# Samples' products with C in four bursts, and half of the state updates behind the next group's first block

## The reference

```python
cum = jnp.cumsum(dt * A, axis=1)
y = jnp.einsum('btsgh,bsghp->btghp', w, x)
y = y + jnp.einsum('btgn,bghpn->btghp', cm, h) * jnp.exp(cum)[..., None]
tail = jnp.exp(cum[:, -1:] - cum) * dt
h_new = jnp.exp(cum[:, -1])[..., None, None] * h + jnp.einsum('bsgh,bsgn,bsghp->bghpn', tail, bm, x)
```

## Time and profile before

| | before |
|---|---|
| median of 3 runs | 1644.11 us (1643.53 to 1644.78) |
| profiled execution | 1640.79 us, span 1639.1 us, clock 0.926 |
| PE busy | 1396.7 us (85%) |
| DVE busy | 1198.9 us (73%) |
| ACT busy | 810.0 us (49%) |
| POOL busy | 214.6 us (13%) |
| block products, line 794 | 3840 records, 293.1 + 280.1 + 279.6 us |

### The profile page before, as it was taken

One profiled execution on the slowest core, in us unless ns is written; L12 is line 12 of the kernel. 1 busy time (PEld: TensorE's weight loads), 2 busy tenths in 40 slices (PEclk: granted clock), 3 DMA queues, 4 the chain that ended last, 5 costly groups with the idle time before them and its releaser, 6 DMA issues. The chain is left out here.

```text
span 1639.1 us, 26283 instructions
## 1 busy us (share of the span) xinstructions
PE 1396.7 (85%) x8709; PEld 1238.2 (76%) x8709; DVE 1198.9 (73%) x1710; ACT 810.0 (49%) x1420; POOL 214.6 (13%) x342
## 2 busy tenths in 40 slices
PE   3899989899998999989893899997349999999980
PEld 2898988888888798888882799985247777777760
DVE  4248787988878888787986454542639999999974
ACT  3136353554635436352541332322038989898961
POOL 0003011030211203012030000000220111111112
PEclk9999998999989899998995999998669999999995
DMA  5033441615325153351632825311269999999936
GB/s 146 19 110 81 117 127 53 186 56 144 98 86 151 52 156 86 103 139 53 171 84 78 272 70 172 113 52 36 91 253 369 366 359 363 356 369 358 364 140 231
DMA packets 191359, 271.53 MB, mean 166 GB/s; under 512 B 15884, under 2 KB 154358, under 8 KB 174886
## 3 DMA queue, kind: packets, MB, share of 16 engines
q1 hardware_dynamic: 178350, 245.62, 45.3%
q0 software_dynamic: 9968, 18.25, 3.1%
q10 hardware_dynamic: 2992, 7.03, 1.2%
HBM read 237.95 MB, written 50.26 MB: 176 GB/s over the span
## 5 line engine op out<-in xcount | busy, mean ns | idle before, releaser
L794 PE MATMUL pu<-xh,wh 128*128 128x304 f32 (+1 forms) x1280 | 293.1, 312 | 31.7 <-DVE wl L236 29.2
L794 PE MATMUL pu<-xl,wh 128*128 128x304 f32 (+1 forms) x1280 | 280.1, 302 | 0.0
L794 PE MATMUL pu<-xh,wl 128*128 128x304 f32 (+1 forms) x1280 | 279.6, 301 | 0.0
L794 PEld LDWEIGHTS pu<-xh,wh 128*128 128x128 f32 x1280 | 208.6, 200 | 47.3 <-DVE wl L236 36.2
L794 PEld LDWEIGHTS pu<-xl,wh 128*128 128x128 f32 x1280 | 208.7, 199 | 0.0
L794 PEld LDWEIGHTS pu<-xh,wl 128*128 128x128 f32 x1280 | 207.0, 199 | 0.0
L914 DVE SCALAR_TENSOR_TENSOR cacc<-a_p,gc,cacc 128x528 f32<-128x528 f32 x232 | 188.9, 814 | 5.8
L2086 DVE TENSOR_TENSOR W13l<-W,W13h 128x1024 fp32r<-128x1024 f32 x160 | 185.0, 1218 | 5.1 <-ACT W13h L2034 5.1
L496 ACT ACTIVATE wh<-ring 128x1024 fp32r<-128x1024 f32 x80 | 84.4, 1056 | 201.9 <-PE pu L794 201.9
L2034 ACT ACTIVATE W13h<-W 128x1024 fp32r<-128x1024 f32 x160 | 156.3, 1063 | 4.8 <-DMA W<-in_exp_w 4.8
L1993 PE MATMUL eh<-W13h,xch 128*128 128x512 f32 x320 | 130.5, 408 | 19.3 <-DVE xcl L2086 14.9
(11 more groups left out here) (397 smaller groups left out, 2694.2 us busy)
## 6 DMA issues: line engine op xcount, KB each, us to landing
W<-in_exp_w SPq DMA_DIRECT2D x120, 1024.0 KB, 7.7
ring<-in_w_in SPq DMA_DIRECT2D x80, 512.0 KB, 4.0
stage<-decay_rows SPq DMA_DIRECT2D x8, 1120.0 KB, 6.8
x<-in_state_ssm SPq DMA_DIRECT2D x16, 512.0 KB, 6.3
out_new_ssm_sample<-x SPq DMA_DIRECT2D x16, 512.0 KB, 5.3
wraw<-in_ssm_out_w SPq DMA_DIRECT2D x8, 1024.0 KB, 8.0
Ed<-decay_rows SPq DMA_DIRECT2D x32, 140.0 KB, 7.2
gates<-gbuf ACTq DMA_DIRECT2D x16, 280.0 KB, 2.1
```

The source lines that it names most:

```text
L794: last = pe.matmul(u_cols(r, a, b), w[:, k % RING, j, :], x[:, j, a:b], start=(j == 0 and n == 0), stop=(j == KD - 1 and n == 2))
```

## The change

1. The 16 products of the samples' states with C leave `stage2(5)`. A new `samples(r)` makes them in four bursts of four, each waiting for its own quarter of `h0T` alone; between bursts stands one of the 8 steps of block 9. The last burst tells VectorE. `block` gets bounds in steps instead of halves.
2. `states_added` for quarters 2 and 3 moves from the end of a group into `closing`, behind the next group's block 0. VectorE's updates of these quarters move behind its split of block 2's weights.
3. In the last group VectorE makes the samples' convolution and two taps before the first updates, with `cv` as room, and five more taps before `scaled`.

```diff
             def closing(g):
 
+                for r in (2, 3):
+                    states_added(g, r)
                 pe.wait_ge(s_y, 6 * g + 6 + 1)
...
-                    if ci == 0:
-                        pe.wait_ge(s_h0tev, 4 * g + 4)
-                        for i in range(2):
-                            for b in range(NSAMP):
-                                last = pe.matmul(pC[:, P * i + TSAMP * b:P * i + TSAMP * b + TSAMP],
-                                                 h0T[:, i, b, :], cv[:, 3, TSAMP * b:TSAMP * b + TSAMP],
-                                                 start=True, stop=True)
...
+                def samples(r):
+
+                    i, q = r // 2, r % 2
+                    pe.wait_ge(s_h0tev, 4 * g + r + 1)
+                    if r == 0:
+                        pe.wait_ge(s_y, 6 * g + 6)
+                    for b in range(4 * q, 4 * q + 4):
+                        c = P * i + TSAMP * b
+                        last = pe.matmul(pC[:, c:c + TSAMP], h0T[:, i, b, :], cv[:, 3, TSAMP * b:TSAMP * b + TSAMP],
+                                         start=True, stop=True)
+                    if r == 3:
+                        last.then_inc(s_pe2, 1)
...
-                block(9, (0,))
+                block(9, 0, 2)
                 states_turned(2)
+                block(9, 2, 4)
                 states_turned(3)
+                samples(0)
+                block(9, 4, 5)
+                samples(1)
+                block(9, 5, 6)
                 stage2(5)
-                block(9, (1,))
-                for r in range(4):
-                    states_added(r)
+                samples(2)
+                block(9, 6, 7)
+                samples(3)
+                block(9, 7)
+                for r in (0, 1):
+                    states_added(g, r)
...
                 split(g, 2)
+                if not is_first:
+                    states_new(g - 1, (2, 3))
...
-                for r in range(4):
-                    dve.wait_ge(s_hs, 4 * g + r + 2)
-                    dve.wait_ge(s_h0t, 4 * g + 4)
-                    for b in range(4):
-                        bb, i = 4 * (r % 2) + b, r // 2
-                        last = stt(h0[:, i, bb, :], h0[:, i, bb, :],
-                                   Ed[:, i, TSAMP * bb + TSAMP - 1:TSAMP * bb + TSAMP],
-                                   turn[r % 2][:, P * b:P * b + P])
-                    last.then_inc(s_hnew, 1)
+                if is_last:
+                    conf_samples(g, cv[:, :, :].rearrange("p q t -> p (q t)"))
+                    conf_taps(g, range(CK - TRAIL, CK - TRAIL + 2))
+                states_new(g, (0, 1))
...
             group(G - 1, is_last=True)
+            states_new(G - 1, (2, 3))
+            conf_taps(G - 1, range(CK - TRAIL + 2, CK - TRAIL + 7))
             scaled(G - 1)
-            conf_samples(G - 1)
-            conf_taps(G - 1, range(CK - TRAIL, CK))
+            conf_taps(G - 1, range(CK - TRAIL + 7, CK))
```

More of the change, by code:

```diff
@@ L756, in _, with states_added @@
             pe.wait_ge(s_dect, 4)
+            def states_added(g, r):
+                pe.wait_ge(s_Bblk, g + 1)
+                if r < 2:
+                    pe.wait_ge(s_h0tev, 4 * g + r + 3)
+                else:
+                    pe.wait_ge(s_hnew, 4 * g + r)
+                i, q = r // 2, r % 2
+                pe.matmul(turn[r % 2][:, :], xtl[0:SAMP, 1, 2 * i:2 * i + 2, :],
+                          Bblk[:, 4 * q:4 * q + 4, :], start=True, stop=True).then_inc(s_hs, 1)
             def closing(g):
+                for r in (2, 3):
+                    states_added(g, r)
                 pe.wait_ge(s_y, 6 * g + 6 + 1)
@@ L782, in free, with block @@
                     pe.wait_ge(s_ufree, U0 + max(r, 1))
-                def block(k, halves=(0, 1)):
+                def block(k, first=0, end=KD):
                     r = U_OF[k]
[L787 to L797, removed]
+                    if first == 0:
+                        free(r)
+                        low_done(pe, g, k)
+                    for j in range(first, end):
+                        for n, (w, x) in enumerate(((wh, xh), (wh, xl), (wl, xh))):
+                            for a, b in ((0, USPLIT), (USPLIT, T)):
+                                last = pe.matmul(u_cols(r, a, b), w[:, k % RING, j, :], x[:, j, a:b],
+                                                 start=(j == 0 and n == 0), stop=(j == KD - 1 and n == 2))
+                    if end == KD:
+                        last.then_inc(s_u, 1)
                 def stage1(j):
@@ L875, in group @@
                     block(k)
[L877 removed]
+                block(6, 0, 4)
                 stage1(0)
                 stage1(1)
[L880 removed]
+                block(6, 4)
                 stage2(0)
                 stage1(2)
[L883 removed]
+                block(7, 0, 4)
                 stage2(1)
                 stage1(3)
[L886 removed]
+                block(7, 4)
                 stage2(2)
                 stage1(4)
[L889 removed]
+                block(8, 0, 4)
                 stage2(3)
@@ L1016, in conf_taps, with states_new, conf_samples @@
                             k.link(ins)
-            def conf_samples(g):
-                    dve.wait_ge(s_yn, 2 * g + 2 + 1)
+            def states_new(g, rs):
+                for r in rs:
+                    dve.wait_ge(s_hs, 4 * g + r + 2)
+                    dve.wait_ge(s_h0t, 4 * g + 4)
+                    for b in range(4):
+                        bb, i = 4 * (r % 2) + b, r // 2
+                        last = stt(h0[:, i, bb, :], h0[:, i, bb, :],
+                                   Ed[:, i, TSAMP * bb + TSAMP - 1:TSAMP * bb + TSAMP],
+                                   turn[r % 2][:, P * b:P * b + P])
+                    last.then_inc(s_hnew, 1)
+            def conf_samples(g, room=None):
+                    if room is None:
+                        dve.wait_ge(s_yn, 2 * g + 2 + 1)
+                        room = ybuf[:, :, :].rearrange("p i t -> p (i t)")
                     n = CK - 1 + TSAMP
```

20 lines of the change are left out of this document (6 added, 14 removed).

## The result

| | predicted | measured |
|---|---|---|
| median | 1648.8 us (1635 to 1660) | 1661.59 us (1661.12 to 1662.49, 4 runs) |
| against before on the same chip (1643.82 us) | +4.7 us | +17.8 us, ratio 1.011 [1.0092, 1.0127] |
| profiled execution | 1645.5 us | 1661.39 us, span 1659.7 us, clock 0.906 (before 0.926) |

The changed kernel is slower, as forecast, but by nearly four times as much (1.1%), and 1.6 us beyond the range. The waits of TensorE in the groups' body come first, by instruction and what ended them: us in total, times, longest.

What follows compares the result with a forecast made beforehand. The hand-over between groups was taken to set the period: seven stretches at 31.3 us instead of 29.6 add 11.9, the last group's end saves 7.2, so +4.7: 1645.5 us profiled, median 3.3 above, 1648.8 us (1635 to 1660).

Steps and rivals of the forecast that it cites:

- What bounds the kernel: Hand-over between groups, from block 9's start to the next block 1: seven stretches of 29.6 us, 207.19 in all.
- The bursts: Samples' products with C between pieces of block 9: 0.91 us each, the 0.39 us wait gone, no clock fall.
- S: Moment when the last burst of samples' products ends, forecast 10.5 us after block 9's start.
- The wait of block 0: TensorE waits before the next group's block 0 for ScalarE to take the last gate: 2.4 us, new.
- The wait of the sums: TensorE waits before its two sums for VectorE's moved updates, behind block 0: 1.9 us more.
- The end: VectorE's work alone after the last group's last burst: 27.4 us, net 7.2 us less.
- The clock: Falls at the two new waits cost 2.9 us a stretch, making it 31.3 us, 1.7 more than before.
- Together 2.9: Clock price per stretch in us: 1.9 in block 0 every group, plus 1.0 for the second wait's fall half the time.
- a wait of 2.5 us alone was enough: Before the change, one TensorE wait of 2.5 us for weights was read as enough to bring the clock down.
- Rival C: Clock falls inside the bursts as well: price 4.9 us, 33.3 a stretch, +18.7, 1662.8 us; chance 0.12.
- Rival A: Clock holds through bursts, mostly falling inside waits: price 0.9 us a stretch, -9.3, 1634.8 us; chance 0.28.
- Rival B: Costs and gains cancel: clock price 2.2 us a stretch, no net change, 1644 us; chance 0.20.

Runs made afterwards that it cites:

- f3: In effect the changed kernel run again, as the intended fill ahead of the sums stands nowhere in the trace: 1660.14 us, ratio 1.0101 to before.
- f2: Changed kernel with 18 unread products of 256 columns (2.42 us) filling the wait ahead of block 0: 1647.09 us, ratio 1.0025 to before.
- g1: Changed kernel with 13 unread products of 256 columns (1.80 us) filling the wait ahead of the sums: 1653.37 us, ratio 1.0058 to before.
- f1: In effect f2 again, a second fill missing from the trace: 1645.66 us, one slow run at 1725.39 left out, ratio 1.0021 to before.
- g2: Changed kernel with unread products filling both waits, ahead of block 0 and ahead of the sums: 1656.68 us, ratio 1.0057 to before.
- e7: Changed kernel with VectorE's moved updates set ahead of its split of block 2: 1640.64 us, ratio 0.9974 to before.
- e2: Kernel before with part 2 alone, plus part 1's separate waits for each quarter ahead of the 16 products: 1644.03 us, ratio 0.9998.
- e1: Changed kernel without part 2, all state products and updates back at the group's end: 1629.96 us, ratio 0.9911; repeated 1628.12 us, 0.9901.
- e4: Changed kernel with block 0 of a next group waiting for its own bank alone: 1643.3 us, ratio 0.9989 to before.
- e6: e4 with state products 2 and 3 behind block 0's second and fourth eighth, all updates at the group's end: 1643.99 us, ratio 1.0003.
- e5: Changed kernel with the edits of both e4 and e7: 1626.87 us, ratio 0.988 to before; repeated 1633.48 us, 0.9933.
- part 3 alone: Kernel before with only VectorE's new order in the last group: 1635.54 us, ratio 0.9949 to before.

## Why the prediction was right in direction and wrong in size

**What bounds the kernel: right.** The hand-over between groups sets the period. Its seven stretches grew by 22.6 us (229.75 against 207.19), most of the 25.7 that the seven groups lost. The middle of a group kept its waits (29.3 us in 14, for 29.2), but not its clock; see below.

**The bursts: right.** No idle time ahead of them, full clock between them, S at 10.56 us for 10.5.

**The wait of block 0: right.** 2.38 for 2.4 us, released by ScalarE's gate, in six of seven; in the first stretch 0.26 was left, as the clock fell ahead of it and the state products took its time. **The wait of the sums: right.** 1.77 for 1.9. VectorE's split ended later (1.23 us from 387.65 on), the updates behind it.

**The end: right.** 27.3 us for 27.4. The last group's block 9 starts 24.5 us later than before (849.15 to 873.63) and the last tap ends 17.3 later (894.22 to 911.51), so the end gave back 7.2 us, the number forecast.

**The clock: this step failed.** The term "Together 2.9" had three faults of size.

| | forecast | in the stretch of the rows above |
|---|---|---|
| fall at the first wait, paid in block 0 | 1.9 us | 8.96 - 6.28 = 2.7 us |
| fall at the second wait, paid in the sums | "half the time the same price, 1.0" | 3.50 - 1.68 = 1.8 us, every time |
| low clock in block 1, behind the stretch | nothing | about 1.1 us, every time (69.5 for 68.4) |

So 4.5 us stands in the stretch where 2.9 was set: 28.3 + 4.5 = 32.8 us, as measured. Behind it another 1.1, which the sum could not see, as the stretch was cut at block 1's start. (The 2.4 us of 394.50:396.90 at half the clock do half their work, so 1.2 us is the upper bound of that share.) Part of this was made up: before, three of the seven pieces behind a stretch lost 1.5 us to the fall behind a wait for weights, and none does now, so these pieces grew by 3.1 us together, not by 7.7.

The whole account, in the two profiled executions: the stretches are 10.7 us longer than forecast (22.6 for 11.9), the pieces behind them 3.1, group 0 comes to its block 9 1.2 us earlier (157.30 for 158.50), and the end is as forecast. That is 12.6 us too little at the last tap, and the forecast of the median was 12.8 too low. The profiled execution came out 15.9 above its forecast; 3.3 us of that lie behind the last tap, where the change touches nothing, and the traced execution of before was itself 3.0 us under its median.

That the clock falls in the second wait was the least certain link, and I priced it by a mean over happening and not happening. It happened seven times of seven, and in the repeat (f3) again. What speaks for the waits as its cause is that filling them, at the same length, took the fall at that place away, in seven of seven stretches of f2 and g1 (six in f1). What speaks against a simple rule is that the fall then came elsewhere, in g1 and g2 as a longer low stretch from the bursts on, and that in the changed kernel itself, and in four groups of e7, the first fall stood ahead of the wait. The prediction's reading that a wait of 2.5 us alone was enough took one place: of the 14 waits for weights seven are of 2.5 us, and in the profiled executions three of these seven have a fall behind them before the change, none after it, and all seven in e2. The step also took "no fall" for the bursts and the work right behind them: that held in six of seven stretches here, and in two of seven of e1.

**Rival C** had the time right (1662.8) and the mechanism wrong: its fall inside the bursts isn't there, they run at 1.00. **Rival A** had the clock hold; it fell twice in each of seven stretches. **Rival B** didn't occur in the changed kernel. e2, e4 and e6 come out level with before, as it had it, but by other sums of waits and clock.

The Trainium skill's "TensorE: Matmul & The Clock Gate", section "Loop structure matters more than you think", shows matmuls losing the high clock to an 8 us wait between them. Here it fell in waits of 2.38 and 1.77 us, each beside sparse products, in 13 of 14 places; at the fourteenth, and in e1, it fell with no wait ahead of it. The direction agrees with the trace; the waits here were much shorter than in its example.

**What stays open.** Why one sequence of work (e5, g2) keeps the clock in some groups and loses it for 10 us or more in others is not settled. The records show where the clock was low and what TensorE did before, not what the chip decides by. No run moved the same work in time without changing it, so whether the moment at which it comes decides is not tested; nor is what the numbers in the unread products do.

## What to carry to other kernels

Price a new wait of TensorE as the wait, plus a fall of the clock behind it where sparse work stands beside it, and follow that fall through every dense instruction behind it, past the edge of the stretch that you sum. Don't take the mean over "falls" and "doesn't": give both sums. In a loop it can come in every pass, as here, or in four of seven (e5). A new wait can also cost nothing (e2). Before moving work to shorten one chain, ask what work covered another engine's chain (here four state products covered ScalarE's gate); try each part alone and in pairs, since their effects did not add up here.

## What the runs showed of the hardware

Three things I had not expected. Sparse work alone can bring TensorE's clock down: in e1 it fell behind bursts of 4-column products and stayed at 1.2 GHz for 13.6 us, through four state products over 32 rows and most of block 0, with TensorE busy for all 13.60 us and for the 5.50 us ahead. Filling a wait of 2.38 us with 2.42 us of products nobody reads made the kernel 14 us faster (f2 against the changed kernel), and filling the second one as well made it no better (g2, 1656.7, against f2's 1647.1). And the parts' effects are far from additive: part 3 alone is -8.4 us, parts 1 and 3 -14.6 to -16.3, part 2 (nearly) alone 0, all three +17.8. Parts 1 and 2 together make the first wait, and the traces show the clock falling in other places in each of these kernels.
